# Latent attention in two halves of four heads, and a value unit of layer 2 computed in layer 1's experts

## What is computed

```python
u = rms_norm(h, norm_mix[l]); proj = u @ w_in[l]
o_a = hgrn2_mixer(...)        # 4 heads, a gated recurrence by chunks of 64 rows
o_b = short_conv_mixer(...)   # a width-3 convolution, then a norm by groups
o_c = mla_mixer(...)          # latent attention, below
h = h + concatenate([o_a, o_b, o_c]) @ w_out[l]
h = h + cross_attention(rms_norm(h), rms_norm(mem), xa_wq, xa_wk, xa_wv, xa_wo)
h = h + hier_moe(rms_norm(h), ...)   # 32 experts, 2 chosen for a row
```

```python
s = (qn @ k_nope + qp @ k_rot) * (64 + 32) ** -0.5
s = where(key_chunk <= query_chunk, s, -1e30)
o = softmax(s) @ v                     # then a norm by heads
```

## Time and profile before

| | |
|---|---|
| median of 3 runs | 857.52 us (856.44 to 858.63) |
| profiled execution | 858.14 us |
| its span | 856.3 us |
| PE busy | 809.4 us, 95% |
| DVE, ACT busy | 389.3 us (45%), 181.5 us (21%) |
| mean granted TensorE clock | 0.978 of full speed |
| DMA | 272.56 MB, mean 318 GB/s |

### The profile page before, as it was taken

One profiled execution on the slowest core, in us unless ns is written; L12 is line 12 of the kernel. 1 busy time (PEld: TensorE's weight loads), 2 busy tenths in 40 slices (PEclk: granted clock), 3 DMA queues, 4 the chain that ended last, 5 costly groups with the idle time before them and its releaser, 6 DMA issues.

```text
span 856.3 us, 13118 instructions
## 1 busy us (share of the span) xinstructions
PE 809.4 (95%) x5588; PEld 550.7 (64%) x5588; DVE 389.3 (45%) x672; ACT 181.5 (21%) x417; POOL 14.4 (2%) x21
## 2 busy tenths in 40 slices
PE   9999999999999999989879999999999999789776
...
GB/s 347 414 254 126 48 308 184 98 385 260 205 293 425 428 425 427 426 427 426 426 420 425 124 51 262 230 121 279 358 210 366 358 430 427 428 427 427 426 420 209
DMA packets 27180, 272.56 MB, mean 318 GB/s; under 512 B 3312, under 2 KB 3824, under 8 KB 9328
## 3 DMA queue, kind: packets, MB, share of 16 engines
...
## 4 chain that ended last, share of the span: by engine, by line
PE 76%; DMA 20%; DVE 2%; ACT 1%; issue 1%; SPq 0%; another core or an unknown queue 0%; DVEq 0%; PEld 0%; PEldq 0%; ACTq 0%
DMA early<-in_expert_units 20%; PE bank L1288 10%; PE bank L763 10%; PE bank L894 8%; PE bank L1141 6%; PE bank L1355 6%; PE bank L934 4%; PE bank L864 3%; PE bank L946 3%; PE bank L1069 3%; PE bank L833 2%; PE bank L1387 2%; PE bank L1368 2%; PE bank L1126 2%; PE bank L1042 1%; PE bank L967 1%
## 5 line engine op out<-in xcount | busy, mean ns | idle before, releaser
L894 PE MATMUL bank<-ring,xT 128*32 128x512 f32 x548 | 67.1, 616 | 15.1 <-DMA ring<-in_expert_units 15.0
L2734 DVE TENSOR_TENSOR hid<-hid,bank 128x256 f32<-128x256 f32 x16 | 6.7, 421 | 148.4 <-ACT hid L1940 148.4
L894 PE MATMUL bank<-early,xT 128*32 128x512 f32 x464 | 59.4, 652 | 13.8 <-DMA early<-in_expert_units 13.7
L946 PE MATMUL bank<-yy,states 128*128 128x512 f32 x112 | 55.0, 620 | 0.0
L894 PEld LDWEIGHTS bank<-ring,xT 128*32 128x32 f32 x548 | 18.1, 111 | 56.4 <-issue 40.7
L2739 DVE COPY yy<-bank 128x512 f32<-128x512 f32 x14 | 9.7, 691 | 97.2 <-PE bank L934 97.2
L864 PE MATMUL bank<-sel,hn 128*128 128x128 f32 x448 | 52.3, 275 | 0.0
L864 PEld LDWEIGHTS bank<-sel,hn 128*128 128x128 f32 x448 | 51.3, 192 | 0.5 <-issue 0.5
L894 PEld LDWEIGHTS bank<-early,xT 128*32 128x32 f32 x464 | 15.0, 115 | 54.6 <-issue 41.7
L763 PE MATMUL bank<-uT,ring 128*128 128x256 f32 x224 | 49.4, 379 | 0.0
L1940 ACT ACTIVATE hid<-bank 128x256 f32<-128x256 f32 x16 | 6.1, 383 | 190.0 <-PE bank L894 190.0
...
## 6 DMA issues: line engine op xcount, KB each, us to landing
ring<-in_expert_units SPq DMA_DIRECT2D x43, 2048.0 KB, 22.8
early<-in_expert_units SPq DMA_DIRECT2D x37, 2048.0 KB, 24.8
ring<-in_fixed_units SPq DMA_DIRECT2D x18, 2048.0 KB, 10.4
ring<-in_fixed_units SPq DMA_DIRECT2D x20, 1024.0 KB, 18.1
early<-in_expert_units SPq DMA_DIRECT2D x11, 1024.0 KB, 38.6
ring<-in_expert_units SPq DMA_DIRECT2D x10, 1024.0 KB, 6.4
...
```

The costliest lines, as they stand in the source:

```text
L894: mm = pe.matmul(bank[2][32 * e:32 * e + 32, :], xT[:, 2 * n + c, 32 * e:32 * e + 32], w_ahead[:, e] if first and n == 0 and c == 0 and e ...
L946: mm = pe.matmul(sums(t, n)[:, :], turned[:, 4 * odd + t], yy[:, n * 512:n * 512 + 512], start=False, stop=False, skip_group_check=True)
```

## The change

1. *Halves.* The latent attention is done for heads 0 to 3 and then for heads 4 to 7. `MLA_SCORES = ((0, 1, 4), (2, 3, 5))` names the scores of each half. PE's order becomes: `mq0`, wait for `out0` and `out1`, `mq1`; `mk0`, `mk1`; `mq2`; the first half's scores; `mq3`, `hgss`, `mv0`, `mv1`; the second half's scores; the first half's transposes; `op1`; `mo0`; the second half's transposes; `mss0`; `mo1`; the first half of `op7`; `mss1`; its second half. The probabilities are divided by their sums in four instructions, and the turned probabilities have a buffer for each half.
2. *Signs and factors.* Keys are copied with the factor -1, so that DVE takes the minimum of the scores and ACT uses it as its bias as it is; the softmax's factor goes into the queries' norm (`eps_q`). DVE's scaling of each maximum goes (6 instructions a layer). The cross attention does the same with its queries (4 a layer).
3. *`op7`* moves from ahead of the transposes to behind the outputs.
4. *The wait for `out0` and `out1`* moves on PE from ahead of `mq3` to behind `mq0`, and DVE makes its first block of them ahead of its work on `mq0`.
5. *`xv3`* of layer 2 is computed in quad 6 of layer 1's experts, and `xv1` moves to quad 5, `xv0` to quad 4, `xk3` to quad 3; `xk2` shares quad 2 with `xk1` (quads count from 0 here, so this is the third). In layer 1's mixer `xv3` stays, in four pieces of four matmuls at other places; in layer 2's mixer nothing stands in its stead. One of SP's rules for the buffers gets an exception, `KEPT_TO_RING`: two units of the last quad but one stay in the ring.

The diff, cut to the orders on the engines; left out are the helpers that only move, the names of buffers and semaphores, the tables of the constants, and what follows of part 2:

```diff
-NEXT_IN_QUAD, NEXT_BEHIND_LAYER = {1: "xk0", 2: "xk1", 3: "xk2", 4: "xk3", 5: "xv0", 6: "xv1"}, ["xv2"]
+NEXT_IN_QUAD, NEXT_BEHIND_LAYER = {1: ["xk0"], 2: ["xk1", "xk2"], 3: ["xk3"], 4: ["xv0"], 5: ["xv1"], 6: ["xv3"]}, ["xv2"]
...
+KEPT_TO_RING = ((EXPERT_UNITS - 6, EXPERT_UNITS - 5), ())
...
-              ("mq2", "V", 2), ("mq3", "V", 4), ("mk0", "A", 5), ("mk1", "A", 6), ("hgss", "A", 3), ("mv0", "A", 7), ("mv1", "A", 0),
-              ("ms0", "A", 1), ("ms1", "A", 2), ("ms2", "A", 3), ("ms3", "A", 4), ("ms4", "A", 5), ("ms5", "A", 6), ("op1", "V", 7), ("op7", "V", 0),
-              ("mt0", "A", 2), ("mt1", "A", 3), ("mt2", "A", 4), ("mt3", "A", 5), ("mt4", "A", 6), ("mt5", "A", 2),
-              ("mo0", "A", 3), ("mo1", "A", 4), ("mss0", "A", 5), ("mss1", "A", 6), ("xv3", "A", 1),
+              ("mk0", "A", 5), ("mk1", "A", 3), ("mq2", "V", 2), ("ms0", "A", 6), ("ms1", "A", 5), ("ms4", "A", 7), ("mq3", "V", 4), ("hgss", "A", 1),
+              ("mv0", "A", 3), ("mv1", "A", 2), ("ms2", "A", 0), ("ms3", "A", 4), ("ms5", "A", 1), ("mt0", "A", 6), ("mt1", "A", 3), ("mt4", "A", 2),
+              ("op1", "V", 7), ("mo0", "A", 5), ("mt2", "A", 6), ("mt3", "A", 3), ("mt5", "A", 2), ("mss0", "A", 4), ("mo1", "A", 6),
+              ("mss1", "A", 5), ("op7", "V", 0), ("xv3", "A", 1),
...
                 latent_queries(0)
+                for n in range(2):
+                    wait_unit(base, f"out{n}")
+                pe.sem_inc(M["half_done"], 1)
                 block_sums("convss", tb("blk64"), cu, "conv_sq", 1)
                 latent_queries(1)
...
-                latent_queries(2)
-                for n in range(2):
-                    wait_unit(base, f"out{n}")
-                pe.sem_inc(M["half_done"], 1)
-                latent_queries(3)
...
+                latent_queries(2)
+
+                def latent_scores(half):
...
+                    pe.wait_ge(M["mla_q"], in_layer(lay, "mla_q", half + 1))
+                    for n in MLA_SCORES[half]:
...
+                latent_scores(0)
+                latent_queries(3)
                 free_unit("mq3")
                 block_sums("hgss", tb("blk64"), kl, "hg_sq", 1)
                 for t in range(T):
...
-                wait_emptied(lay, "mk1")
-                pe.wait_ge(M["mla_k"], in_layer(lay, "mla_k", 1))
-                pe.wait_ge(M["mla_q"], in_layer(lay, "mla_q", 1))
-                for n in range(4):
-                    o = begin(f"ms{n}")
...
                 free_unit("mv1")
+                latent_scores(1)
...
+                turn_latent_probabilities(0)
                 pe.wait_ge(M["mixed"], in_layer(lay, "mixed", 2))
                 row_product(begin("op1"), uT[:, 0:4, P:S], w11).then_inc(pe_job, 1)
+                for n in range(2):
+                    wait_unit(base, f"xq{n}")
+                latent_outputs(0)
+                if lay == 0:
+                    wait_unit(base, "xv3")
+                    begin("xv3")
+                later_values(0, 4)
+                turn_latent_probabilities(1)
+                block_sums("mss0", tb("blk64"), mqT[:, 4:6], "mla_osq", 1)
+                later_values(4, 8)
+                latent_outputs(1)
                 proj_made(3)
-                row_product(begin("op7"), proj_s3, w12).then_inc(pe_job, 1)
-                wait_unit(base, "xv3")
-                v3 = begin("xv3")
-                part_of_values("xv3", v3, lay, 0, 1)
-
-                pe.wait_ge(M["mla_p"], in_layer(lay, "mla_p", 1))
-                for n in range(4):
-                    o = begin(f"mt{n}")
...
-                    mm.then_inc(pe_job, 1)
-                part_of_values("xv3", v3, lay, 1, 4)
-                after("mt5")
-                for n in range(2):
-                    o = begin(f"mo{n}")
-                    wait_unit(base, f"xq{n}")
...
-                part_of_values("xv3", v3, lay, 4, 6)
-                for n in range(2):
-                    block_sums(f"mss{n}", tb("blk64"), mqT[:, 4 + 2 * n:6 + 2 * n], "mla_osq", n + 1)
-                part_of_values("xv3", v3, lay, 6, 2 * KC).then_inc(pe_job, 1)
+                o = begin("op7")
+                row_product(o, proj_s3, w12, chunks=range(2))
+                later_values(8, 12)
+                block_sums("mss1", tb("blk64"), mqT[:, 6:8], "mla_osq", 2)
+                row_product(o, proj_s3, w12, chunks=range(2, 4)).then_inc(pe_job, 1)
+                later_values(12, 2 * KC)
 
                 pe.wait_ge(M["mixed"], in_layer(lay, "mixed", 3))
                 proj_made(5)
                 row_product(begin("op4"), uT[:, 4:8, 0:P], w12, onto=True).then_inc(pe_job, 1)
-                free_unit("xv3")
+                if lay == 0:
+                    free_unit("xv3")
...
-                    name = NEXT_IN_QUAD.get(q) if lay == 0 else None
-                    if name is not None and q + 1 != DRAIN:
-                        pe.wait_ge(next_gained, 1)
-                        fill_next(name, base)
+                    names = NEXT_IN_QUAD.get(q, []) if lay == 0 else []
+                    if q + 1 != DRAIN:
+                        for name in names:
+                            pe.wait_ge(next_gained, 1)
+                            fill_next(name, base)
...
+                latent_exponentials(0)
                 group_rstd("hgss", flat(ql), 64, M["hg_rstd"])
                 for t in range(T):
                     copy_out(f"mv{t}", mV[:, t])
...
-                    group_rstd(f"mss{n}", mkT[:, 2 * n:2 * n + 2].rearrange("p c s -> p (c s)"), 64, M["mla_rstd"])
-                keep_memory(lay, "xv3")
+                latent_exponentials(1)
+                keep_turned_latent(0)
+                keep_latent_outputs(0)
+                keep_turned_latent(1)
+                group_rstd("mss0", flat(mkT[:, 0:2]), 64, M["mla_rstd"])
+                keep_latent_outputs(1)
+                group_rstd("mss1", flat(mkT[:, 2:4]), 64, M["mla_rstd"])
+                if lay == 0:
+                    keep_memory(lay, "xv3")
...
+                dve.wait_ge(M["half_done"], in_layer(lay, "half_done", 2))
+                make_proj(proj_t1, w12, w11, ALU.subtract)
+                turn_latent_queries(0)
...
                 turn_latent_queries(1)
+                dve.wait_ge(dve_emptied, emptied(lay, "mq1"))
+                dve.sem_inc(M["mla_q"], 1)
...
-                dve.wait_ge(M["half_done"], in_layer(lay, "half_done", 2))
-                make_proj(proj_t1, w12, w11, ALU.subtract)
-                turn_latent_queries(2)
-                turn_latent_queries(3)
-                dve.wait_ge(dve_emptied, emptied(lay, "mq3"))
-                dve.sem_inc(M["mla_q"], 1)
                 proj_made(1)
                 make_proj(w12, w22, w12, ALU.subtract)
...
-                dve.wait_ge(M["hg_rstd"], in_layer(lay, "hg_rstd", 1))
-                st(dve.tensor_tensor(flat(uT[:, 0:2]), flat(gate), flat(ql), ALU.mult))
-                settle()
-                dve.sem_inc(M["mixed"], 1)
...
                     settle()
-                    st(dve.tensor_reduce(small[:, x:x + per], o, AX.X, ALU.max))
+                    dve.tensor_reduce(small[:, x:x + per], o, AX.X, ALU.min).then_inc(M["mla_neg"], 1)
+
...
+                for at in range(3):
+                    lowest_latent_score(0, at)
+                turn_latent_queries(2)
+                turn_latent_queries(3)
+                dve.wait_ge(dve_emptied, emptied(lay, "mq3"))
+                dve.sem_inc(M["mla_q"], 1)
+                scale_latent_probabilities(0, 1)
+                lowest_latent_score(1, 0)
+                scale_latent_probabilities(0, 0)
+                dve.wait_ge(M["hg_rstd"], in_layer(lay, "hg_rstd", 1))
+                st(dve.tensor_tensor(flat(uT[:, 0:2]), flat(gate), flat(ql), ALU.mult))
+                settle()
+                dve.sem_inc(M["mixed"], 1)
+                lowest_latent_score(1, 1)
+                lowest_latent_score(1, 2)
+                make_proj(proj_s3, r11, r21, ALU.subtract)
+                scale_latent_probabilities(1, 1)
+                scale_latent_probabilities(1, 0)
                 gone(dve.tensor_tensor(h[:, 1, 0:D // 2], h[:, 1, 0:D // 2], job("op1")[:, :], ALU.add))
                 make_proj(w11, w22, proj_t1, ALU.subtract)
                 gone(dve.tensor_tensor(h[:, 0, D // 2:D], h[:, 0, D // 2:D], job("op7")[:, :], ALU.add))
```

228 lines of the change are left out of this document (122 added, 106 removed).

## The result

The changed kernel takes 883.23 us (median of 4 runs, 880.67 to 883.45) beside 858.04 for the kernel before in the same comparison: a ratio of 1.029 (95% interval 1.0265 to 1.0314), 25 us slower. Forecast were 878 us and a range of 867 to 885. Its profiled execution has a span of 881.2 us, 24.9 more than before; PE is busy 814.5 us (809.4 before).

A forecast was written before the change was run, and what follows sets the result against it. Transfers bound layer 1's experts, PE's work layer 2's latent stretch. 858.14 + 0.5 (layer 2's mixer) + 10.0 (layer 1's mixer) + 6.4 (layer 1's experts) + 3.4 (clock) = 878.4, less 0.6: 878 us, range 867 to 885.

The forecast's parts named there:

- The end of the mixer: Behind op7, ahead of op4: PE waits for VectorE's chain, 5.3 us in layer 1 and 4.8 in layer 2.
- `out1`: Layer 1, behind the first latent queries: PE waits 3.0 us for out1 to land.
- The sign that it would be put down to a DMA: Layer 1, behind the first latent queries: the profile would put PE's 3 us of idle time down to a DMA.
- The middle: Latent attention's outputs: PE waits 1.7 us at mo0 in both layers; in layer 2 also 0.25 at mss0, 0.7 at mo1.
- Layer 2's mixer: Layer 2's mixer: 7.45 us of new waits for 6.9 us of xv3's work removed, +0.5 us.
- The clock: Behind the waits after op7 in both layers: half clock costs 1.7 us each, +3.4 us; none for layer 1's 3.0 us wait.
- Layer 1's experts: Layer 1's expert stage: 2.45 us for one more 1024 KB unit plus 3.9 of lost transfers, +6.4 us.
- the drought's term: Layer 1's experts, third quad: two fills give buffers back late, the DMA queue runs dry, 3.9 us of transfers lost.
- the faster one: Rival, both mixers: the halves cover each other, new waits, clock and dry queue under 4.5 us; 853 us, chance 0.04.
- Swallowed: Rival, layer 1's experts: the mixer's 10.0 us delay vanishes in PE's idle time there; 866 us, chance 0.07.
- The milder case: Rival, layer 1's experts and mixers: the queue stays fed and the clock at 1.00; 870.5 us, chance 0.22.

The follow-up runs named there:

- three remedies: Changed kernel with op7 ahead of the outputs, the wait for out0 and out1 and VectorE's blocks of them later, the first fill's buffer given back early: 864.11 us.
- busy matmuls: Changed kernel with matmuls of no use ahead of op4, five in layer 1 and four in layer 2: 877.28 us.
- first experiment: Changed kernel with PE's wait for out0 and out1 behind the recurrence's change of state and VectorE's first block of them behind mq1: 883.05 us.
- halves alone: Changed kernel with xv3 back as filler in layer 2's mixer and one unit in each quad of layer 1's experts as before: 881.13 us.
- `xv3` alone: Kernel before with layer 2's xv3 moved and the new table of units in layer 1's experts, latent attention as before: 863.49 us, ratio 1.0068.

## Why the prediction was right, and where its terms were off

*The end of the mixer: right.* 4.8 us forecast in layer 2, 4.62 measured; 5.3 in layer 1, 5.10. It was read off four durations of the earlier trace rows. Moving `op7` back took it away in layer 1 (0.69 is left); in layer 2 other waits, 1.35 and 2.41 us, came up in its stead.

*`out1`: right in idle time, short by its clock.* 3.0 forecast, 3.21 measured. The prediction gave that wait no clock; the 5.39 us of PE's work behind it run at 0.50, which is 2.7 us (2.68 us from the norm to the change of state before). The sign that it would be put down to a DMA did not come: the profile says `issue`. This is the largest of the terms that made 878 too low.

*The middle: right where it was large.* 1.7 at `mo0`, measured 1.65. The 0.25 at `mss0` and 0.7 at `mo1` came out as 0.33 together; the two waits of 0.30 us ahead of `hgss` and the second scores were not seen.

*Layer 2's mixer: +0.5 forecast, +1.69 measured.* The idle time was right (7.45 against 7.21). The saving was not: PE's busy time fell by 5.52 us and not by 6.9. The same shortfall stands in layer 1 without any slow clock, 40.66 against 39.59 for the same records. The halves make more and shorter runs of like matmuls, and I take the 1.1 to 1.4 us to be the changes between them. The rows fit this: counted to the next start, less idle time, layer 1 of the three remedies has 0.25 us more than before in `xv3` (7.36 for 7.11), 0.21 in the outputs (3.03 for 2.82), 0.16 in the values and at most 0.10 in each other job. But no run changes the number of runs alone, so the cause is argued, not tested.

*The clock: right in kind, too small.* Two drops at 1.7 us gave 3.4; measured are 2.40 and 2.49 behind `op4` and 2.7 behind `out1`, 7.6 in all. The busy matmuls show the first two as the clock's; the third goes with its wait: in the first experiment, without the wait there, the work from the norm to the change of state takes 2.68 us again (119.07 to 121.75). The step of the sum that failed is there: "none for the 3.0 us wait in layer 1". The sizes hold for this trace only. Behind waits at the same places the same work took between 5.23 and 5.96 us (`op4` in layer 1: halves alone, the changed kernel) and between 4.35 and 5.39 (behind `out1`: the same two).

*Layer 1's experts: +6.4 forecast, +3.4 measured.* The queue did run dry where the prediction has it, and the late load took 7.8 us. Mis-sized is the drought's term: 3.9 us forecast, 1.6 of transfers lost in the changed kernel and 1.7 with `xv3` alone. The prediction has both buffers back together, and the issue at 323.5; in the kernel with `xv3` alone, where the stage begins where it did before, the first load is issued at 321.23, 2.3 us earlier, and the second at 323.58. With the unit's 2.45 the lost transfers make some 4.1. The stage's growth scatters around that: 3.4 in the changed kernel, where it begins 17 us later, 5.7 with `xv3` alone, 6.0 in the first experiment, where it begins 12.7 us later, 3.2 with the busy matmuls, where it begins 13.6 us later. Its length doesn't follow its beginning in these runs, and what sets it within these 3 us is open.

*Sum.* The span grew by 24.9 us where the terms made 20.3. Too low were the clock by 4.2, layer 1's latent stretch by 0.6 of idle time and 1.5 of work (4.19 us of added busy time less the clock's 2.7), layer 2's by 1.2, and what is ahead of that by 0.2; too high were the experts by 3.0: 4.7 in all, to rounding the 4.6 that are missing. So the mechanisms are the forecast's own, and all that it named came, in kind. That the time lies 5 us above the forecast and not 8, and so inside the range, is luck in part: the drought came out small where the clock came out large. Of the rivals, the faster one failed where the prediction put it: all new waits, the clock and the drought come to far more than 4.5 us. "Swallowed" was wrong: the experts begin 17 us later and are longer, not shorter. In the first experiment 2.6 us of a gain in layer 1's mixer were lost again in the experts, but with the busy matmuls the stage begins 3.5 us earlier, too, and takes 206.6; so that loss lies within the stage's scatter and doesn't show that it gives gains back. The milder case had the queue and the clock wrong, though its queue was nearer to the 1.6 us than the 3.9 were.
